# A hybrid encoder layer on one core: the mixers of the next block placed between the FFN's matmul groups

## The reference

```
z = RMSNorm(x) @ W_in                               # 1024 -> 1536 columns
A = silu(LayerNorm(causal_conv31(za * sigmoid(zg))))     # 256 channels, 31 taps
B = attention(RMSNorm(q), RMSNorm(k), v)            # 8 heads of 64, 2 kv heads; a chunk of 64
                                                    # queries reads 192 keys; bias table, sinks
C = z * sigmoid(z @ w_glu),  z = gelu(Re(C h) + D u)     # diagonal complex state, scanned over time
x = x + concat(RMSNorm(A), RMSNorm(B), RMSNorm(C)) @ W_out
h = RMSNorm(x)
x = x + (silu(causal_conv3(h @ W_gate)) * (h @ W_up)) @ W_down
```

## Time and profile before

| | us |
|---|---|
| median of three runs | 2697.62 |
| the profiled execution | 2698.67 |
| its span | 2696.9 |
| PE busy | 2425.0 (90%) |
| DVE busy | 1343.9 (50%) |
| ACT busy | 1008.5 (37%) |
| POOL busy | 1285.7 (48%) |

### The profile page before, as it was taken

One profiled execution on the slowest core, in us unless ns is written; L12 is line 12 of the kernel. 1 busy time (PEld: TensorE's weight loads), 2 busy tenths in 40 slices (PEclk: granted clock), 3 DMA queues, 4 the chain that ended last, 5 costly groups with the idle time before them and its releaser, 6 DMA issues. The chain is left out here.

```text
span 2696.9 us, 35680 instructions
## 1 busy us (share of the span) xinstructions
PE 2425.0 (90%) x13157; PEld 2201.4 (82%) x13157; DVE 1343.9 (50%) x1815; ACT 1008.5 (37%) x1691; POOL 1285.7 (48%) x875
## 2 busy tenths in 40 slices
PE   5888772869899768999999999999999999999997
PEld 5888771324555468999999999999999999999997
DVE  1297797933897425434254242542425424266371
ACT  4432311114454524335244342443424434243341
POOL 2333238201453045655555556555555555666562
PEclk9998896979999879999999999999999999999998
DMA  4342230020000043434444344443444434443339
GB/s 88 101 109 70 86 54 5 0 1 13 3 0 0 0 112 103 133 102 133 130 133 133 100 132 132 133 133 99 130 134 133 133 98 133 134 132 122 105 122 68
DMA packets 194475, 248.42 MB, mean 92 GB/s; under 512 B 104006, under 2 KB 148714, under 8 KB 194346
## 3 DMA queue, kind: packets, MB, share of 16 engines
q1 hardware_dynamic: 186106, 246.66, 33.4%
q10 hardware_dynamic: 8240, 0.03, 0.2%
HBM read 237.84 MB, written 8.91 MB: 91 GB/s over the span
## 5 line engine op out<-in xcount | busy, mean ns | idle before, releaser
L669 POOL TENSOR_TENSOR ffn_w_lo<-z_t,ffn_w_hi 128x1024 fp32r<-128x1024 f32 (+1 forms) x340 | 900.7, 2650 | 552.5 <-ACT ffn_w_hi L728 515.1
L121 PE MATMUL ffn_bank<-ffn_mov_hi,ffn_w_hi 128*128 128x416 f32 x2080 | 735.1, 353 | 27.1 <-DVE ffn_mov_lo L807 21.2
L123 PE MATMUL ffn_bank<-ffn_mov_hi,ffn_w_lo 128*128 128x416 f32 x2080 | 734.3, 353 | 0.0
L122 PE MATMUL ffn_bank<-ffn_mov_lo,ffn_w_hi 128*128 128x416 f32 x2080 | 728.7, 350 | 0.0
L728 ACT ACTIVATE ffn_w_hi<-z_t 128x1024 fp32r<-128x1024 f32 (+1 forms) x340 | 385.9, 1136 | 607.5 <-PE ffn_bank L123 385.0
L121 PEld LDWEIGHTS ffn_bank<-ffn_mov_hi,ffn_w_hi 128*128 128x128 f32 x2080 | 392.1, 188 | 31.3 <-issue 27.8
L123 PEld LDWEIGHTS ffn_bank<-ffn_mov_hi,ffn_w_lo 128*128 128x128 f32 x2080 | 392.0, 188 | 5.3
L122 PEld LDWEIGHTS ffn_bank<-ffn_mov_lo,ffn_w_hi 128*128 128x128 f32 x2080 | 391.7, 188 | 4.5
L877 DVE TENSOR_TENSOR ffn_h_lo<-z_t,ffn_h_hi 128x416 fp32r<-128x416 f32 x110 | 283.5, 2577 | 118.0 <-ACT ffn_h_hi L779 118.0
L121 PE MATMUL ffn_bank<-ffn_h_hi,ffn_w_hi 128*128 128x416 f32 x880 | 312.2, 355 | 5.2 <-DVE ffn_h_lo L877 4.3
L122 PE MATMUL ffn_bank<-ffn_h_lo,ffn_w_hi 128*128 128x416 f32 x880 | 310.8, 353 | 0.0
(11 more groups left out here) (330 smaller groups left out, 2776.2 us busy)
## 6 DMA issues: line engine op xcount, KB each, us to landing
z_t<-in_w_gate_up_t SPq DMA_DIRECT2D x220, 512.0 KB, 3.5
z_t<-in_w_down_t SPq DMA_DIRECT2D x80, 704.0 KB, 4.1
pin_w_raw<-in_w_in SPq DMA_DIRECT2D x96, 256.0 KB, 3.2
z_t<-in_w_out_t SPq DMA_DIRECT2D x40, 512.0 KB, 3.7
z_t<-in_x_t SPq DMA_DIRECT2D x40, 208.0 KB, 2.6
out_y_t<-z_t SPq DMA_DIRECT2D x40, 208.0 KB, 4.2
pin_x<-in_x_prompt SPq DMA_DIRECT2D x4, 2048.0 KB
att_logit<-bias_by_distance SPq DMA_DIRECT2D x8, 48.0 KB, 2.5
```

The costliest lines, as they stand in the source:

```text
L121: pe.matmul(out, w_hi, x_hi, start=first, stop=False)
L122: pe.matmul(out, w_hi, x_lo, start=False, stop=False)
L123: return pe.matmul(out, w_lo, x_hi, start=False, stop=last)
L669: pool.tensor_tensor(w_lo[n % RING_W][:, 0:size], raw[n % 2][:, 0:size], w_hi[n % RING_W][:, 0:size].bitcast(F32), ALU.subtract).then_inc( ...
```

## The change

- `attend`, `norm_groups` and `out_ffn` become one phase, `encode_blocks`. Its column blocks are 384, 448, 448, 384 and 416 wide (6, 7, 7, 6, 6 query chunks, the last with the 32 columns of the old stream).
- The conv leaves `project_in` and `ssm_run`. In their place `ssm_prepare` stores the conv's inputs, q, k and v (10 DMAs of SP) and `ssm_run` the output of the state mixer (10 DMAs) to a tensor in memory, `z_spill`. `encode_blocks` loads them block by block.
- The mixers of a block (conv, norms of q and k, attention, group norms) are a list of steps r (class `When`). For block 0 the steps 0 to 59 run ahead of the first matmul group, a new query chunk every 2 steps. For block b + 1 step r stands on every engine behind group r of the FFN of block b, counted from its first gate group, with a new chunk every 5 steps: the loads at steps 0 and 8, the 62 conv taps at 7 to 37 (two a step, DVE L1157, L1159, the running sum in the residual's SBUF buffer), the norms of q and k from 12 to 19, the first scores at 21, LayerNorm and norm of A from 38 to 51, the norm of B to 60 or 68.
- The hidden tiles go in four parts (5, 5, 6, 6) instead of two of 11, so a block has 32 down groups of 5 or 6 k-tiles, and there are 420 groups. `RING_P` is 3, the five other banks serve the mixers.
- A chunk's division moves from POOL to DVE (L1261); scores multiply rows of 64 instead of zero-padded ones of 128; values are transposed on PE chunk by chunk (L1404 to L1406); constants come in one DMA, `new_ffn_conv` leaves in one.

```diff
+FCH = ((0, 5), (5, 10), (10, 16), (16, NF))
...
-RING_P = 4
+RING_P = 3
...
+class When:
...
+    conv, load_a, load = 7, 0, 8
+    c_norm, qk, scores = 10, 12, 21
+    a_norm = 38
...
+        mixers_at = {at[("gate", b, 0)] + r: (b + 1, r) for b in range(NBLK - 1) for r in range(when[b + 1].end)}
...
-            conv = Conv(Z, S, s_tap, 0, CONV_BEGUN, OW - CONV_BEGUN)
-            conv.first(dve)
...
-            conv.taps(dve, 1, TAPS[0])
...
-                for s, name in enumerate(("new_ffn_conv_p", "new_ffn_conv_s")):
...
+            sp.dma_start(out["new_ffn_conv"], carry[:].rearrange("p f s t -> p (f s t)")).then_inc(s_y, 16)
...
+                if n in mixers_at:
+                    mixers(*mixers_at[n])
...
-            attend(nc, w, Z, ident, taps, rel_rows, out)
-            norm_groups(nc, w, Z, ident)
-            out_ffn(nc, w, Z, out)
...
+        encode_blocks(nc, w, spill, rel_rows, ident, out)
```

More of the change, by code:

```diff
@@ L264, in pe_wait, with project_in @@
         pe.wait_ge(self.s_lo, n + 3)
[L267 to L320, removed]
+def project_in(nc, w, Z, ident, s5_inputs):
     with ExitStack() as ctx:
@@ L561, in out_ffn @@
[L561 to L568 removed]
+        h_hi = m.sb("h_hi", [P, FMAX, NMAX], F32R)
+        h_lo = m.sb("h_lo", [P, FMAX, NMAX], F32R)
@@ new lines, in encode_blocks @@
+        xn = hidden
+        carry = m.sb("carry", [P, NF, 2, 2])
+        ones, pair = m.sb("ones", [P, P]), m.sb("pair", [P, P])
+        eps = m.sb("eps", [P, 1])
+        abuf = m.sb("abuf", [P, 2, PAD + NMAX])
+        kraw = m.sb("kraw", [P, NMAX])
+        kbuf, vbuf = m.sb("kbuf", [P, WINDOW + NMAX]), m.sb("vbuf", [P, WINDOW + NMAX])
+        qn = m.sb("qn", [P, QT * NMAX])
+        ksam = m.sb("ksam", [P, KEYS_S])
+        v_cache = m.sb("v_cache", [P, P])
+        v_one, v_two = ([m.sb(f"v_{n}{i}", [P, P]) for i in range(4)] for n in ("one", "two"))
@@ L782, in _ @@
+            act.wait_ge(s_const, 16)
+            act.wait_ge(s_relps, 1)
+            act.activation(rel[:], vb[0:NHQ, 0:NREL], ACT.Copy).then_inc(s_rel, 1)
+            for r in range(when[0].end):
+                mixers(0, r)
             for n in range(2):
                 weights(n)
+            split_mixed(0)
             for n in range(NG + 2):
@@ L938, in _ @@
+            pe.wait_ge(s_rel_in, 32)
+            pe.matmul(vb[0:NHQ, 0:NREL], table[:], hot[:], start=True, stop=True).then_inc(s_relps, 1)
+            pe.wait_ge(s_made, 15)
+            for r in range(when[0].end):
+                mixers(0, r)
+            for n, (kind, b, i) in enumerate(seq):
+                group(n)
                 if kind == "pout" and b == 0 and i == KD - 1:
                     statistics(0)
-                if kind == "down" and i == (1, 3) and not is_last(b):
+                if kind == "down" and i == (NCHUNK - 1, 3) and not is_last(b):
@@ L1370, in _ @@
             ins.then_inc(s_fin, 1)
-            conv.taps(dve, TAPS[0], TAPS[1])
             for c in range(5):
```

1458 lines of the change are left out of this document (705 added, 753 removed).

## The result

After the change an execution takes 2729.11 us, the median of four runs (2726.37 to 2733.03); four runs of the kernel before beside it have 2698.80 (2696.58 to 2700.75). The ratio is 1.0114, with an interval of 1.0100 to 1.0128: slower by 1.1%, where 0.3% was forecast.

A forecast was written before the change was run, and what follows sets the result against it. PE was taken to bound the FFN. 2696.9 us less 403.5 removed plus 297.5 added gave 2591; 114 us of stalls made 2705, forecast as 2706 us, with an 8-in-10 range of 2620 to 2785.

The forecast's parts named there:

- What goes: Time removed: the stretch 634 to 971, conv in `project_in` and `ssm_run`, and the end of the span; together 403.5 us.
- block 0: Block 0's mixers run alone ahead of the first matmul group: 125 us taken, 88 to 150 possible.
- The tail: End of the span behind the last sum: 5.5 us instead of 16 with one plain DMA, so 10.5 us less.
- (3): PE's attention inside the FFN: 27 chunks at 5.2 us, 140 us, plus sums of 28 us.
- (4): Steps 7 to 37: DVE instructions reading two SBUF tiles and POOL's weight rests exclude one another; 68 us stall, between 5 and 121.
- (5): Change of block: down groups do not cover the chain to the next gate; 8.1 us four times, 32 us, 20 to 50.
- the signs: What would show the forecast in PE's waits: DVE named, with the scaling ahead of each block's first gate some 8 us four times.
- (6): PE's clock falls to the lower level behind stall gaps: four or five gaps, 10 us, 0 to 30.
- (7): Loads of a block's mixers at step 8 delay a weight in the queue: 4 us, 0 to 25.
- The cover that holds: Rival in the FFN: most of DVE's other work lies beside weight rests; 57 us of stalls, 2649 us, chance 0.33.
- The exclusion that wins: Rival in steps 7 to 37: no other DVE work overlaps weight rests; 121 us there, 2759 us, chance 0.19.
- The third: Rival: block 0 takes 150 us instead of 125, each of 27 chunks loses 1 us more; 2758 us, chance 0.06.

The follow-up runs named there:

- the quarter of POOL's work: The changed kernel with POOL making its weight rests for a quarter of the columns only, the others zero: 2635.14 us, 0.9783 of the kernel before.
- after: The changed kernel itself, against the kernel before: 2729.11 us, ratio 1.0114.
- the third run: The changed kernel with ACT making the next block's first gate weights ahead of the scaling at a change of block: 2734.19 us, 1.0153 of the kernel before.
- the hidden tile first: The changed kernel with ACT copying the high hidden tile ahead of the weights of two groups on: 2701.50 us, 1.0037 of the kernel before.

## Why the prediction was right, and where it fell short

The direction was right, the range held the time, and the time is 23 us above the forecast. The direction hung on little: the forecast lay 3 us above what would have counted as no change. Step by step:

- **What goes, and block 0.** The rotation moved 58.9 us (26 + 30 forecast), the first pout came at 706.6 (705). Block 0 alone is near what was forecast, with a chain of idle engines behind its taps; that it is so near is in part luck, as the same steps end up to 13 us later where the clock is lower. The tail took 2.4 us instead of 5.5, which had the landing of a y store, 4.2, behind the last issue; the last store needs less.
- **Attention and sums on PE, (3).** 185 us against 168. A chunk costs 5.4 us where 5.2 were forecast and a sum 0.4 where 0.7 were, together 161; the term left out that the first pass behind each stop is longer, 24 us.
- **The exclusion, (4).** The mechanism is shown by the quarter of POOL's work; its size in the tap steps is 56 us against 68 forecast. That is a lower figure, as the short rests still lengthen the taps (0.74 us where the shortest takes 0.67). Counted in after itself, PE loses 63 us in these stretches, 47 in waits and 16 at the lower clock. The worst place was the one named, steps 14 to 19 under down groups, and the four stretches of taps lose 12.7, 13.7, 3.7 and 25.6 us, where 24, 9, 4 and 31 were forecast. The runs without taps and with moved taps put it to taps and reciprocals meeting there. PE's waits name what was foretold: the additions and the hidden rests; those for scores and probabilities are the same lag of DVE, and go with the taps.
- **The change of block, (5).** 35.2 us in four waits against 32. Right in size, but the waits name POOL's weights and not the scaling, as the signs had it, and the cause in the sum was one of two: ACT's late weights, and the bank that DVE frees behind its scaling. So the forecast would have misled whoever wanted to mend it, as the third run shows.
- **The step that failed.** No term stood for the ends of the hidden parts behind step 37. The forecast took (4) for steps 7 to 37 alone and let "lag" be worked off behind them. But at all four ends of parts PE stops for the last hidden rest: 20 waits, 33 us, of which 16 lie in steps 7 to 37 and 17 outside, where the forecast has nothing. DVE's lag behind its taps is not what makes these 17, since the run without taps has the same 14.0 us behind step 37. By block the 33 are 9.8, 3.6, 4.4, 12.1 and 3.1; the two large ones are the blocks of 384 columns, whose passes are the shortest. With 11 k-tiles to a part the down group of before had ten tiles in hand while the last one was made, and PE waited 4.3 us in all; with 5 or 6 it has four or five, 2 to 3 us of passes, and a hidden rest that first has to wait for a weight rest of 2.4 us comes later than that. That fits the two runs that take this wait away: with rests on a quarter 7.2 of the 33 us are left, with the hidden tile first 14.1. The row of `ffn_h_lo` at 2.58 us was read, but only as a price for the taps; it was not asked what covered it where the change itself cuts the cover.
- **The clock and the loads, (6) and (7).** 10 us were forecast at the lower clock for four or five gaps; there are some 40 waits, and 28 us more than before, of which some 13 lie outside the tap steps. For the loads 4 us were forecast, and no wait of PE in the FFN names a DMA.
- **The sum.** The error of 23 us is thus in the main (3), 17 too low, and the ends of parts, 17; against them (4), the loads and the tail came out 3 to 5 us lower each.
- **The rivals.** The cover that holds, 57 us of stalls, is refuted: there are some 125. The exclusion that wins, with (4) at 121, is too: 56 to 63. The third, with the first pout 25 us later and a chunk 1 us dearer, is refuted by 706.6, and by the run without taps, in which the chunks' waits are gone. The forecast of 114 is low by a tenth.

## What to carry to other kernels

Work put beside a stretch that one engine bounds must be summed stage by stage, in the few microseconds of one step, with engines that exclude each other added and not laid side by side; mean busy shares of 50% hid steps where DVE and POOL together needed 7.5 us and PE 3. When a reduction is cut into shorter parts or a bank is given away, every chain that ran behind the long part loses cover: list those chains first. Where two engines exclude one another, the order in which a third releases them is worth trying before any work is removed: one pair of swapped copies gave back 28 us, and moved taps 34.

## What was not expected of the hardware

A tap of 32 columns cost 0.63 us beside weight rests and 0.33 with rests of a quarter: it lost 0.30 us, nearly as much as one of 448 columns (0.37), so many small instructions pay for the exclusion much as large ones do. And the first pout, at 706.6 us in after, came as late as 719.3 in a kernel that differs in block 0 by the buffers of the roots alone: PE's granted clock between 640 and 685 us was 0.84 in the one and 0.50 in the other.
